# A layer norm and the modulation behind it folded into one factor and one offset per channel, and the router's logits moved into the norm

## What is computed

```
def layer_norm_2(x, g, b):
    mu = x.mean(-1, keepdims=True)
    var = jnp.square(x - mu).mean(-1, keepdims=True)
    return (x - mu) * lax.rsqrt(var + LN_EPS) * g + b
def modulate(x, shift, scale):
    return x * (1 + scale) + shift
def ffn_sublayer(x, shift, scale, gate, w_gu, w_down, g, b):
    y = swiglu(modulate(x, shift, scale), w_gu, w_down)
    return layer_norm_2(ALPHA * x + 0.5 * gate * y, g, b)
# second block, per layer, for x (256 tokens) and ctx (256 tokens):
#   x = ffn_sublayer(x, ...); h = modulate(x, ...); o = mixer(h, h_ctx)
#   x = layer_norm_2(ALPHA * x + gate * o, ...); x = ffn_sublayer(x, ...)
# first block, the router of the experts:
aff = jax.nn.sigmoid(xt @ router_w)     # 1024 x 16, then groups and top k
```

## Time and profile before

| what | us |
|---|---|
| median of 3 runs | 3422.85 |
| lowest and highest | 3418.06 and 3425.38 |
| profiled execution, its own time | 3427.45 |
| its span, first to last instruction | 3425.4 |
| PE busy | 3171.5 |
| VectorE busy | 1628.0 |
| ScalarE busy | 1053.5 |

### The profile page before, as it was taken

How to read it: one execution, slowest core, us unless ns; L and a number is a source line. 1 busy time by engine, 2 the same in 40 slices (tenths; PEclk the granted TensorE clock), 3 DMA queues, 4 the chain that set the end, 5 groups by cost and what they waited for, 6 DMA issues and landing times.

```text
span 3425.4 us, 42182 instructions
## 1 busy us (share of the span) xinstructions
PE 3171.5 (93%) x17332; PEld 2522.5 (74%) x17332; DVE 1628.0 (48%) x2548; ACT 1053.5 (31%) x1609; POOL 10.6 (0%) x41
## 2 busy tenths in 40 slices
PE   8899999989999899998988878899998999987898
PEld 7678876777877688884446777478886888755898
DVE  1545486245458732433955665243335333314554
ACT  1333375234347622212032111132224212212333
POOL 0000000000000000000000000000000000000000
PEclk9899999999999999998988987999999999988999
DMA  6347696435779522223130002222221222220352
GB/s 229 153 150 282 262 361 262 163 140 197 276 288 356 209 98 98 92 81 127 71 139 35 25 26 111 86 74 98 98 98 62 95 90 98 74 74 1 135 184 99
DMA packets 69107, 479.30 MB, mean 140 GB/s; under 512 B 7376, under 2 KB 10832, under 8 KB 11728
## 3 DMA queue, kind: packets, MB, share of 16 engines
q1 hardware_dynamic: 67616, 473.16, 37.2%
q10 hardware_dynamic: 1328, 3.85, 0.3%
HBM read 475.93 MB, written 1.05 MB: 139 GB/s over the span
## 4 chain that ended last, share of the span: by engine, by line
PE 71%; PEld 8%; DVE 7%; issue 5%; ACT 4%; PEldq 2%; DMA 2%; ACTq 0%; DVEq 0%; SPq 0%
PE ps L528 18%; PE ps L529 17%; PE ps L530 17%; PEld ps L520 7%; PE ps L520 4%; PE ps L1368 1%; PE ps L787 1%; PE ps L1656 1%; PE ps L1966 1%; PE ps L1982 1%; PE ps L1383 1%; ACT X L818 1%; PE ps L1664 1%; DMA ring<-in_moe_up 1%; PE ps L1981 1%
## 5 line engine op out<-in xcount | busy, mean ns | idle before, releaser
L549 DVE TENSOR_TENSOR w_lo<-ring,w_hi 128x1024 fp32r<-128x1024 f32 x552 | 671.7, 1224 | 732.2 <-ACT w_hi L541 726.2
L541 ACT ACTIVATE w_hi<-ring 128x1024 fp32r<-128x1024 f32 x552 | 582.1, 1058 | 919.2 <-PE ps L530 769.5
L528 PE MATMUL ps<-x_hi,w_hi 128*128 128x512 f32 (+1 forms) x1408 | 515.4, 366 | 41.0 <-DVE x_lo L694 39.0
L529 PE MATMUL ps<-x_lo,w_hi 128*128 128x512 f32 (+1 forms) x1408 | 514.1, 365 | 0.0
L530 PE MATMUL ps<-x_hi,w_lo 128*128 128x512 f32 (+1 forms) x1408 | 513.7, 365 | 0.0
L528 PEld LDWEIGHTS ps<-x_hi,w_hi 128*128 128x128 f32 x1408 | 268.4, 191 | 86.0 <-issue 41.0
L520 PE MATMUL ps<-HM,ring 128*128 128x256 f32 (+1 forms) x928 | 300.2, 485 | 19.2 <-DVEq L857 13.5
L530 PEld LDWEIGHTS ps<-x_hi,w_lo 128*128 128x128 f32 x1408 | 268.3, 191 | 42.0
L529 PEld LDWEIGHTS ps<-x_lo,w_hi 128*128 128x128 f32 x1408 | 268.6, 191 | 41.5
L520 PEld LDWEIGHTS ps<-HM,ring 128*128 128x128 f32 x928 | 180.1, 195 | 136.5 <-issue 118.2
L529 PE MATMUL ps<-h_lo,w_hi 128*128 128x512 f32 (+1 forms) x704 | 255.2, 363 | 0.0
(11 more groups left out here) (386 smaller groups left out, 4707.4 us busy)
## 6 DMA issues: line engine op xcount, KB each, us to landing
ring<-in_moe_up SPq DMA_DIRECT2D x128, 1024.0 KB, 5.4
ring<-in_ff_up SPq DMA_DIRECT2D x88, 1024.0 KB, 4.7
ring<-in_ada SPq DMA_DIRECT2D x72, 1024.0 KB, 4.9
ring<-in_moe_down SPq DMA_DIRECT2D x64, 1024.0 KB, 5.3
ring<-in_ff_down SPq DMA_DIRECT2D x44, 1024.0 KB, 4.7
ring<-in_w_in SPq DMA_DIRECT2D x14, 1024.0 KB, 6.6
ring<-in_even_in SPq DMA_DIRECT2D x10, 1024.0 KB, 4.8
ring<-in_w_o SPq DMA_DIRECT2D x8, 1024.0 KB, 8.3
```

Of the source, the lines that this page charges most:

```text
L528: pe.matmul(dst, hi, xh, start=start, stop=False, skip_group_check=True)
L529: pe.matmul(dst, hi, xl, start=False, stop=False, skip_group_check=True)
L541: act.activation(w_hi[:, j % HALVES, :], ring[:, u % SLOTS, (j % 2) * D:(j % 2 + 1) * D], ACT.Copy)\
L549: dve.tensor_tensor(w_lo[:, j % HALVES, :], ring[:, u % SLOTS, (j % 2) * D:(j % 2 + 1) * D], w_hi[:, j % HALVES, :].bitcast(F32), ALU.subt ...
```

## The change

At four norms of the second block (b2.0.ln1, b2.0.ln2, b2.1.ln0, b2.1.ln1) norm gain and bias and the modulation are one factor and one offset per channel, FOLD, made by `fold_norm` in an earlier stage. After the inverse, VectorE writes V = Y * factor * inverse (`folded_dve`), ScalarE writes x_hi = V + offset (`folded_act`), and VectorE x_lo = V + offset - x_hi. X, the plain output of the norm, is still needed for the residual; it is made afterwards (`keep_scaled_dve`, `keep_x_act`). PE goes into the next stage's matmuls without `enter`. For b2.1.ln0 the target is HM, and the first output chunk of `in3_pe` waits for it chunk by chunk. In the first block the modulation's products and the logits are moved into `ln_pe`, with router_w as the stationary operand, and come out turned; Exp is taken on 16 rows and two small transposes turn the result back.

```
+        FOLDED = {"b2.0.ln1": (0, 0, 6, 7, "b2.0.ffn1"), "b2.0.ln2": (1, 1, 0, 1, "b2.1.ffn0"),
+                  "b2.1.ln0": (2, 1, 3, 4, None), "b2.1.ln1": (3, 1, 6, 7, "b2.1.ffn1")}
+        FOLD_IN = {"b2.0.ffn0": ["b2.0.ln1"], "b2.0.ffn1": ["b2.0.ln2"], "b2.1.ffn0": ["b2.1.ln0", "b2.1.ln1"]}
...
-        def ln_stage(name):
-            st = stage(name, pe=["mean", "var"], act=[*[f"sq{k}" for k in range(DC)], "inverse"],
+        def ln_stage(name, logits=False):
+            st = stage(name, pe=["mean", "var"] + ["logits"] * logits,
+                       act=[*[f"sq{k}" for k in range(DC)], "inverse"] + [f"affine{k}" for k in range(DC * logits)],
...
         def ffn_pe(pe, name, n, xh, xl, hh, hl):
-            st = enter(pe, name)
+            st = stages[name] if name in FED else enter(pe, name)
...
-            both = st.modulated and n == N2
+            both = st.modulated and n == N2 and name not in FED
             if both:
                 act.wait_ge(mod_ready, l + 1)
                 second_half(0)
-            for k in range(DC):
+            if name in FED:
+                tables_silu(act)
+                keep_x_act(act, FED[name], n)
+            for k in range(DC if name not in FED else 0):
...
+            if name in FED:
+                keep_scaled_dve(dve, FED[name], n)
+                dve.wait_ge(x_kept, DC * (kept_at[FED[name]] + 1))
+            else:
...
             link(dve.tensor_scalar(Y[:, :, 0:n], X[:, :, 0:n], ALPHA, None, ALU.mult))
+            for site in FOLD_IN.get(name, ()):
+                fold_norm(dve, link, site)
...
+            if "logits" in st.names["pe"]:
+                modulation(pe, name, site_banks[name])
+                for k in range(DC):
+                    pe.wait_ge(act_done, st.v("act", f"affine{k}"))
+                    ins = pe.matmul(ps[0:E_N, 6, 0:T], router_w[:, k, :], X[:, k, 0:T], start=(k == 0), stop=(k == DC - 1))
+                ins.then_inc(pe_done, st.one("pe", "logits"))
...
+            if name in FOLDED:
+                folded_act(act, name, n)
+                act.drain().then_inc(act_done, 1)
+                return
...
             for k in range(DC):
                 act.wait_ge(dve_done, st.v("dve", f"scaled{k}"))
                 ins = act.activation(X[:, k, 0:n], Y[:, k, 0:n], ACT.Identity, scale=col(g, k), bias=col(b, k))
+                if "affine0" in st.names["act"]:
+                    ins.then_inc(act_done, st.one("act", f"affine{k}"))
...
+            if name in FOLDED:
+                folded_dve(dve, name, n)
+                dve.drain().then_inc(dve_done, 1)
+                return
...
+        def fold_norm(dve, link, name):
+
+            at, l, shift, scale, _ = FOLDED[name]
+            dve.wait_ge(mod_ready, l + 1)
+            g, b = [inner(col(f"ln{x}{name[-1]}{name[3]}", 0, DC), 2) for x in "gb"]
+            dve.tensor_tensor(FOLD[:, at, 0, :, :], MD[:, l, scale, :, :], g, ALU.mult)
+            link(dve.tensor_tensor(FOLD[:, at, 1, :, :], MD[:, l, scale, :, :], b, ALU.mult))
+            link(dve.tensor_tensor(FOLD[:, at, 1, :, :], FOLD[:, at, 1, :, :], MD[:, l, shift, :, :], ALU.add))
+
...
+        def folded_act(act, name, n):
+            st = stages[name]
+            at, feeds = FOLDED[name][0], FOLDED[name][4]
+            V_ = VM if feeds else HM
+            for k in range(DC):
+                act.wait_ge(dve_done, st.v("dve", f"scaled{k}"))
+                for part, c in halves_of(n):
+                    to = x_hi[:, k, c] if feeds else HM[:, k, c]
+                    ins = act.activation(to, V_[:, k, c], ACT.Identity, bias=FOLD[:, at, 1, k, part:part + 1])
+                ins.then_inc(xhi_done if feeds else hm_done, 1)
...
+        def folded_dve(dve, name, n):
+            st = stages[name]
+            at, feeds = FOLDED[name][0], FOLDED[name][4]
+            V_ = VM if feeds else HM
+
+            def low(k):
+                dve.wait_ge(xhi_done, stages[feeds].x0 + k + 1)
+                for part, c in halves_of(n):
+                    ins = dve.scalar_tensor_tensor(x_lo[:, k, c], V_[:, k, c], FOLD[:, at, 1, k, part:part + 1],
+                                                   x_hi[:, k, c].bitcast(F32), ALU.add, ALU.subtract)
+                ins.then_inc(xlo_done, 1)
+
+            for k in range(DC):
+                for part, c in halves_of(n):
+                    ins = dve.scalar_tensor_tensor(V_[:, k, c], Y[:, k, c], FOLD[:, at, 0, k, part:part + 1], row[:, 0, c],
+                                                   ALU.mult, ALU.mult)
+                ins.then_inc(dve_done, st.one("dve", f"scaled{k}"))
+                if feeds and k > 1:
+                    low(k - 2)
+            if feeds:
+                low(DC - 2)
+                low(DC - 1)
...
+        def keep_scaled_dve(dve, name, n):
+
+            for k in range(DC):
+                dve.tensor_tensor(Y[:, k, 0:n], Y[:, k, 0:n], row[:, 0, 0:n], ALU.mult).then_inc(y_scaled, 1)
+
+        def keep_x_act(act, name, n):
+
+            g, b = [f"ln{x}{name[-1]}{name[3]}" for x in "gb"]
+            for k in range(DC):
+                act.wait_ge(y_scaled, DC * kept_at[name] + k + 1)
+                act.activation(X[:, k, 0:n], Y[:, k, 0:n], ACT.Identity, scale=col(g, k), bias=col(b, k)).then_inc(x_kept, 1)
...
-            rw = cols[:, COLS["rw"][0]:COLS["rw"][0] + DC * E_N].rearrange("p (k e) -> p k e", k=DC)
+            pe.wait_ge(act_done, st.v("act", "exp"))
             for t in range(TT):
-                ins = dot(pe, ps[:, t, 0:E_N], [(X[:, k, tile(t)], rw[:, k, :]) for k in range(DC)])
+                ins = pe.transpose(ps[:, t, 0:E_N], row[0:E_N, 0, tile(t)], ident[0:E_N, 0:E_N])
...
+            act.activation(row[0:E_N, 0, 0:T], ps[0:E_N, 6, 0:T], ACT.Exp, scale=-1.0).then_inc(act_done, st.one("act", "exp"))
             for k in range(DC):
                 act.activation(m_hi[:, k, :], X[:, k, 0:T], ACT.Copy).then_inc(xhi_done, 1)
-            act.wait_ge(pe_done, st.v("pe", "logits"))
-            act.activation(R[:, 0, :].rearrange("p (t e) -> p t e", t=TT), ps[:, 0:TT, 0:E_N], ACT.Exp, scale=-1.0)\
-               .then_inc(act_done, st.one("act", "exp"))
...
-            dve.wait_ge(act_done, st.v("act", "exp"))
+            dve.wait_ge(pe_done, st.v("pe", "logits"))
...
-            link(dve.tensor_scalar(flat(0), flat(0), 1.0, None, ALU.add))
+            link(dve.tensor_scalar(te(0), ps[:, 0:TT, 0:E_N], 1.0, None, ALU.add))
...
         def in3_pe(pe, n):
-            st = enter(pe, n)
+            st = stages[n]
+
+            def chunk(c, k):
+                if c == 0:
+                    pe.wait_ge(hm_done, k + 1)
+                return HM[:, k, :]
+
...
-                dot(pe, ps[:, c % 8, 0:m], [(wt[:, o + k * P:o + (k + 1) * P], HM[:, k, 0:m]) for k in range(DC)])\
+                dot(pe, ps[:, c % 8, 0:m], ((wt[:, o + k * P:o + (k + 1) * P], chunk(c, k)[:, 0:m]) for k in range(DC)), DC)\
...
-                idle(act, act_done, n + "mod1")
+                if l == 0:
+                    idle(act, act_done, n + "mod1")
+                else:
+                    enter(act, n + "mod1")
+                    keep_x_act(act, n + "ln0", N2)
+                    act.drain().then_inc(act_done, 1)
...
-                tables_silu(act)
...
-                modulate(dve, n + "mod1", l, 3, 4)
+                if l == 0:
+                    modulate(dve, n + "mod1", l, 3, 4)
+                else:
+                    enter(dve, n + "mod1")
+                    keep_scaled_dve(dve, n + "ln0", N2)
+                    dve.drain().then_inc(dve_done, 1)
...
-                modulation(pe, n + "ln1", site_banks[n + "ln1"])
...
-                idle(pe, pe_done, n + "mod1")
+                if l == 0:
+                    idle(pe, pe_done, n + "mod1")
+                else:
+                    pe.drain().then_inc(pe_done, 1)
```

More of the change, by code:

```diff
@@ L249, in build @@
         SQ = Space(4096).take(DC, N2)
+        VM = Space(12288).take(DC, N2)
         s = Space(11264 + 2 * DC * SPLIT_SLOTS)
@@ L390, in ffn_stage @@
             count["f"] += (DC - 1) * len(segments)
-            count["q"] += DC if modulated and n == N2 else 0
+            count["q"] += DC if modulated and n == N2 and name not in FED else 0
             c, h = 0, st.h0
@@ L515, in unit_here, with dot @@
             return ring[:, u % SLOTS, :]
-        def dot(pe, dst, pairs):
+        def dot(pe, dst, pairs, count=None):
             for n, (a, b) in enumerate(pairs):
-                ins = pe.matmul(dst, a, b, start=(n == 0), stop=(n == len(pairs) - 1))
+                ins = pe.matmul(dst, a, b, start=(n == 0), stop=(n == (count or len(pairs)) - 1))
             return ins
@@ new lines, in halves_of @@
+        def halves_of(n):
+            return [(part, slice(part * T, (part + 1) * T)) for part in range(n // T)]
+        def folded_act(act, name, n):
[8 more added lines that the diff above has]
```

(1 more changed line is left out.)

27 lines of the change are left out of this document (14 added, 13 removed).

## The result

The changed kernel takes 3394.12 us (median of 3 runs, 3390.31 to 3397.75), the kernel before 3422.85: ratio 0.9916, 95% interval 0.9902 to 0.9929, so 28.7 us faster. Forecast were 3400.5 and a range of 3391 to 3410. The profiled execution of the changed kernel is one of 3390.31, with a span of 3388.2.

A forecast was written before the change was run, and what follows sets the result against it. TensorE bounds the kernel, so gain must come from PE standing still or at lower clock. 7.0 + 7.0 + 4.1 + 7.2 - 3.0 = 22.3 us, from the median 3422.85 to 3400.5; range 3391 to 3410.

The forecast's parts named there:

- A: Gap from b2.0.ln1 to ffn1: PE starts 7.0 us sooner, with the keeping of X hidden; gain 7.0.
- B: Gap from b2.0.ln2 to b2.1.ffn0: same order as A, with two sites to fold; gain 7.0 us.
- The hidden chain: In A, behind the last x_lo: table load, X, ALPHA X, folds, first hidden chunk; ends 2248.3, before PE's 2250.1.
- The covers of 1.8 and 1.2: Time in us by which the chain of X ends before PE's third pair, in A and B respectively.
- C: Gap from b2.1.ln1 to ffn1, 256 columns: new wait of about 1 us before PE's third pair; gain 4.1.
- D: Gap from b2.1.ln0 through mod1 to in: ScalarE paces first output chunk; gain 5.5 to 8.9, middle 7.2 taken.
- Routers: Both b1 layers: logits move ahead, m_hi and m_lo then delay the routing arithmetic by 1.4 and 2.3; cost 3.0 us.
- The sign for SP's loads: In the routers, SP's moe_up loads come 1 to 2 us later against the logits' start.
- The rival with both logits at the low clock: Routers: logits at half clock, arithmetic 3.1 and 5.6 us late; total gain 16.6, 3406 us; chance 0.17.
- the clock stays up: Rival at the four gaps: PE starts at 2.4 GHz after shorter idle; gain 28.5, 3394 us; chance 0.17.
- VectorE at 0.48: Rival: two-scalar operations 0.48 us apart; A 6.2, B 5.6, C 2.8; total gain 18.8, 3404 us; chance 0.12.
- The low clock in the feed: Rival: PE fed piecewise stays at 1.2 GHz; loss 10.5, 3433 us; chance 0.03 loss, 0.05 within 0.2%.

The follow-up runs named there:

- the table loads: Four more loads of ScalarE's tables ahead of the writes of X in A, B and C, against the changed kernel: 3412.57 us, 20.3 over it.
- the repeat: The changed kernel measured again, nothing edited: 3392.23 us, ratio 0.9909 to the kernel before.

## Why the prediction was right, and where it was off

*The bound.* Right: PE's busy time didn't change, and all the gain is time in which it stood or ran low.

*A and B, 7.0 each.* Measured 6.9 and 6.9. The two-scalar operations came 0.40 apart, PE stood 4.8. The hidden chain was put 26.2 behind the inverse and was 25.8 behind it. The covers of 1.8 and 1.2 were 2.1 and 1.2 by the table loads.

*C, 4.1.* Measured 4.4. The new wait came where it was placed, 0.6 for 1. That it is this small is in part the clock's doing: it fell ahead of the wait. The prediction kept PE's old pace, low clock included, and had no case in which PE keeps its clock, waits 1.9 and loses it behind the wait, which would have made 2.9 of 4.4.

*D, 7.2.* Measured 10.2, beyond its bound of 8.9: the term that was mis-sized. The step that failed is "ScalarE paces it: two operations of 0.50 a chunk". An affine with an offset alone was 0.41 apart, and with the second operand 0.50 again and the copies 1.16 later, though that run's stage length of D gave the 1.16 back. The other 1.7 is the middle between the bounds: the low clock lay inside the first output chunk, which the feed paced anyway (keeping PE at 2.4 GHz there gave only 0.6), so the upper bound, not the middle, was right.

*Routers, a cost of 3.0.* It was priced at the start of the routing arithmetic, 1.4 and 2.3 less 0.7. There the two profiles show 0.8 and 1.6: the arithmetic began 3.6 behind the logits in both layers, not 3.95. At the experts' first matmul it was 3.5, at the next norm 1.0, and in the totals nothing. The prediction had all that follows hang on the routing arithmetic one for one; by these profiles the experts' part gave most of it back. The sign for SP's loads, 1 to 2 later against the logits' start, was 2.6 and 2.4. The rival with both logits at the low clock had the right levels, but no run had it in both layers and the prediction's 5.1 and 3.5 were the two levels (5.31, 3.63).

*The sum.* 22.3 forecast, 28.3 in the four stretches and 0 for the routers measured; the medians differ by 28.7 and, with the repeat, 31.3. The missed 6 are D's 3.0 and the routers' 3.0, and both lie on the same side. The measured 28.7 is within 0.2 of what the rival "the clock stays up" would have given (28.5); that is chance, since the clock did fall in A, B and D and A and B gave 6.9, not 8.8 and 8.2.

*The rivals.* VectorE at 0.48 fell by its rows. The low clock in the feed fell too: 5.5 us at 0.50 behind the start in A and then 1.00. The Trainium skill's "TensorE: Matmul & The Clock Gate", section "Why this matters for your kernels", warns of loops with a long wait for data between matmuls. The waits of this feed are short: in the run with PE kept busy, PE was fed in pieces from 2229.45, shows as busy for all of 5.55 us and stayed at 1.00. So the trace doesn't contradict the page, but the warning doesn't reach this feed. What dropped the clock here were gaps of 2.8 to 4.8 without work, the one of 2.8 not in every profile. "The clock stays up" was tried: A +1.6 and B +1.0 for the 1.8 and 1.2 given, D +0.6 for 1.7. The table load cost 1.29 to 1.30 of ScalarE's time in each of 15 cases (the run with four more loads), from its start to that of the next load or write. The 2.66 of the Trainium skill's "ScalarE: Activation LUTs", section "What ACT_TABLE_LOAD costs", isn't seen here: the load alone agrees, no drain shows behind it.

*Open.* Why the experts' part of the second layer is 2.1 shorter in the changed form. What makes b2.0.ln1 begin anywhere from 2194 to 2209: in part the logits' 1.68, and, in stretches whose code is the same in all the changed kernels, the start of the first norm (181.9 to 188.4), the stretch from b1.0.ln2 to b1.1.ln1 (188.9 to 195.4) and that from b2.0.ln0 to b2.0.ln1 (667.3 to 670.6); what varies in them wasn't looked into. And why D's attention lost a spell of low clock in one kernel and became 1.4 longer in another, whose low clock in D is 3.4 less in sum but lies elsewhere.

## What to carry to other kernels

When a pass is moved off the way to the first matmul, follow it to its next reader and give its cover in us: here 2.1, 1.2 and none, in the same code at three sizes and places. Low clock ahead of a wait that another engine ended cost nothing here (C 205.76), and low clock behind it cost 1.5 (C 207.28). So take the wait away first and keep the clock second: keeping PE busy gave 1.7 in the four stretches with the wait in C, and 4.4 with it gone (1173.8 to 1169.4). To tell changes of 0.1 us, compare stage lengths inside the profiles, not totals that scatter by 10.
